# FFN up projection: weights as the loaded operand, tokens as the streamed one

## The reference, cut to what matters

```
D_FF, FFN_CONV = 5632, 3
hn = rmsnorm(h, norm_ffn_w)                       # 256 x 2048
up = causal_dwconv(hn @ w_up, conv_w, conv_b)     # w_up: 2048 x 11264, 3 taps along the tokens
gate, val = jnp.split(up, 2, axis=-1)
h = h + (jax.nn.silu(gate) * val) @ w_down        # w_down: 5632 x 2048
return rmsnorm(h, final_norm_w)
```

## Time and profile before

| | |
|---|---|
| median of 3 runs | 3444.38 us |
| the profiled execution | 3444.65 us |
| its span in the trace | 3442.9 us |
| TensorE matmul busy | 3421.1 us, 99% |
| VectorE busy | 2153.8 us, 63% |
| ScalarE busy | 1647.0 us, 48% |
| first up matmul to first down matmul | 2696.33 to 3194.21 us |

### The profile page before, as it was taken

How to read it: one execution, slowest core, us unless ns; L and a number is a source line. 1 busy time by engine, 2 the same in 40 slices (tenths; PEclk the granted TensorE clock), 3 DMA queues, 4 the chain that set the end, 5 groups by cost and what they waited for, 6 DMA issues and landing times.

```text
span 3442.9 us, 44116 instructions
## 1 busy us (share of the span) xinstructions
PE 3421.1 (99%) x16186; PEld 2791.2 (81%) x16186; DVE 2153.8 (63%) x2573; ACT 1647.0 (48%) x2159; POOL 218.6 (6%) x407
## 2 busy tenths in 40 slices
PE   8999999999999999999999999999999999999999
PEld 6777877778888877888888888888888888888887
DVE  5657577768687657565467774656545566666544
ACT  6442244543354245545555554444444566566433
POOL 1010100101100100100011000000000000000000
PEclk9999999999999999999999999999999999999999
DMA  9987635556867735657777676765655666666665
GB/s 377 398 288 270 223 123 187 176 186 234 271 201 247 272 114 183 235 189 213 216 235 235 211 237 206 250 215 188 206 168 158 186 185 185 186 185 183 202 195 166
DMA packets 331822, 738.85 MB, mean 215 GB/s; under 512 B 26423, under 2 KB 27025, under 8 KB 328448
## 3 DMA queue, kind: packets, MB, share of 16 engines
q1 hardware_dynamic: 298496, 620.83, 56.7%
q0 software_dynamic: 30640, 106.22, 8.7%
q10 hardware_dynamic: 2512, 9.45, 0.8%
HBM read 691.19 MB, written 45.21 MB: 214 GB/s over the span
## 4 chain that ended last, share of the span: by engine, by line
PE 98%; DVE 1%; ACT 1%; DMA 0%; issue 0%; POOL 0%; ACTq 0%; DVEq 0%; POOLq 0%
PE psum L734 30%; PE psum L736 29%; PE psum L735 29%; PE psum L1262 1%; PE psum L1281 1%; PE psum L560 1%; PE psum L1270 1%; PE psum L1325 1%; PE psum L2467 1%; PE psum L1310 0%; PE psum L806 0%; PE psum L2109 0%; PE psum L2277 0%; PE psum L2264 0%; PE psum L1966 0%; PE psum L1247 0%
## 5 line engine op out<-in xcount | busy, mean ns | idle before, releaser
L631 DVE TENSOR_TENSOR w_lo<-w_raw,w_hi 128x1024 fp32r<-128x1024 f32 x997 | 1217.5, 1224 | 1101.8 <-ACT w_hi L623 1099.1
L623 ACT ACTIVATE w_hi<-w_raw 128x1024 fp32r<-128x1024 f32 x997 | 1052.3, 1059 | 1283.2 <-PE psum L736 1169.7
L734 PE MATMUL psum<-w_hi,a_hi 128*128 128x512 f32 x3072 | 1216.0, 396 | 0.8 <-DVE w_lo L631 0.8
L736 PE MATMUL psum<-w_hi,a_lo 128*128 128x512 f32 x3072 | 1198.1, 390 | 0.0
L735 PE MATMUL psum<-w_lo,a_hi 128*128 128x512 f32 x3072 | 1196.4, 389 | 0.0
L734 PEld LDWEIGHTS psum<-w_hi,a_hi 128*128 128x128 f32 x3072 | 577.5, 188 | 122.9 <-issue 7.0
L736 PEld LDWEIGHTS psum<-w_hi,a_lo 128*128 128x128 f32 x3072 | 577.0, 188 | 122.4
L735 PEld LDWEIGHTS psum<-w_lo,a_hi 128*128 128x128 f32 x3072 | 577.7, 188 | 115.8
L734 PE MATMUL psum<-w_hi,f_hi 128*128 128x512 f32 x704 | 276.0, 392 | 0.0
L736 PE MATMUL psum<-w_hi,f_lo 128*128 128x512 f32 x704 | 274.2, 390 | 0.0
L735 PE MATMUL psum<-w_lo,f_hi 128*128 128x512 f32 x704 | 273.9, 389 | 0.0
(11 more groups left out here) (388 smaller groups left out, 2800.7 us busy)
## 6 DMA issues: line engine op xcount, KB each, us to landing
w_raw<-w_in SPq DMA_DIRECT2D x416, 512.0 KB, 4.4
ada_raw<-w_ada SPq DMA_DIRECT2D x176, 512.0 KB, 6.2
w_raw<-ffn_w_up SPq DMA_DIRECT2D x176, 512.0 KB, 3.7
w_raw<-w_out SPq DMA_DIRECT2D x96, 512.0 KB, 4.5
w_raw<-ffn_w_down SPq DMA_DIRECT2D x88, 512.0 KB, 4.8
p<-stage POOLq DMA_DIRECT2D x152, 256.0 KB, 4.8
w_raw<-xa_w_k SPq DMA_DIRECT2D x32, 512.0 KB, 9.6
w_raw<-xa_w_v SPq DMA_DIRECT2D x32, 512.0 KB, 8.4
```

The source lines that it names most:

```text
L623: nc.scalar.activation(w_hi[:, slot], raw_of(k), ACT.Copy).then_inc(hi_ready, 1)
L631: nc.vector.tensor_tensor(w_lo[:, slot], raw_of(k), w_hi[:, slot].bitcast(F32), ALU.subtract).then_inc(lo_ready, 1)
L734: nc.tensor.matmul(acc, g.hi[:, tt, kt, :], w_hi[:, slot, kk, :], start=first, stop=False)
L736: mm = nc.tensor.matmul(acc, g.lo[:, tt, kt, :], w_hi[:, slot, kk, :], start=False, stop=last)
```

## The change

The up product gets a loop of its own in `up_pe`. For a piece it makes 24 matmuls: for each of four blocks of 128 output features and each of two row blocks, a 128x128 block of the weight piece (`w_hi` or `w_lo`) is loaded, and the 256 tokens of `f_hi` or `f_lo` are streamed, as two runs of 128. Two feature blocks share a bank, 256 columns each. The output has features on partitions. The transposes of `turn` are gone, as are its waits on ScalarE and on the convolution.

ScalarE's two copies per chunk are gone. At the end of a chunk VectorE multiplies each of the two banks (128x512) with `rs_row`, a row of the 256 token factors repeated on all partitions, into `stage`. The convolution reads `stage` instead of banks 4 to 7. `rs_row` is made once, in the first chunk: VectorE spreads each tile's factors over 128 columns, TensorE transposes the two squares into bank 4, VectorE copies the bank.

```diff
+        rs_row = at("rs_row", 206.25, [P, SEQ])
+        rs_spread = at("rs_spread", 202, [P, XT, P])
...
+        def up_half(c, f):
+            return stage[:, bank_of(UP, c, f // 2), 256 * (f % 2):256 * (f % 2) + 256]
...
 # ScalarE, conv and body
-                        act.wait_ge(ff_T, i * 4 + (2 * c + f // 2 + 1))
+                        act.wait_ge(acc_evac[bank_of(UP, c, f // 2)], evacs_of(UP, i, c, f // 2) + 1)
...
-                        nc.scalar.activation(y_ff[:, c, f, :], half(4 + 2 * c, f), ACT.Identity, bias=cw[:, c, 3, f:f + 1],
+                        nc.scalar.activation(y_ff[:, c, f, :], up_half(c, f), ACT.Identity, bias=cw[:, c, 3, f:f + 1],
...
-                    for tt in range(XT):
-                        bank = bank_of(UP, c, tt)
-                        wait_unit(act, UP, i, c, tt)
-                        if not first:
-                            act.wait_ge(ff_T, i * 4 - 4 + 2 * c + 2)
-                        nc.scalar.activation(stage[:, bank], psum[:, bank], ACT.Copy, scale=ffn_rs[:, 12 + tt:13 + tt]).then_inc(acc_evac[bank], 1)
 # VectorE, conv and body
-                            ins = nc.vector.scalar_tensor_tensor(y_ff[:, c, f, s:SEQ], half(4 + 2 * c, f)[:, 0:SEQ - s],
+                            ins = nc.vector.scalar_tensor_tensor(y_ff[:, c, f, s:SEQ], up_half(c, f)[:, 0:SEQ - s],
...
+                        if first and c == 0 and j == UP.per_chunk - 1:
+                            dve.wait_ge(late_done, 3)
+                            for tt in range(XT):
+                                ins = nc.vector.tensor_copy(rs_spread[:, tt], ffn_rs[:, 12 + tt:13 + tt].to_broadcast([P, P]))
+                            ins.then_inc(ff_row, 1)
                         split_lo(dve, UP, i, c * UP.per_chunk + j)
                         next(steps, None)
+                    if first and c == 0:
+                        dve.wait_ge(ff_row, 2)
+                        link(nc.vector.tensor_copy(rs_row[:], psum[:, 4, 0:SEQ]))
+                    for pair in range(2):
+                        bank = bank_of(UP, c, pair)
+                        wait_unit(dve, UP, i, c, pair)
+                        nc.vector.tensor_tensor(stage[:, bank].rearrange("p (f q) -> p f q", f=2), psum[:, bank].rearrange("p (f q) -> p f q", f=2),
+                                                rs_row[:].unsqueeze(1).to_broadcast([P, 2, SEQ]), ALU.mult).then_inc(acc_evac[bank], 1)
 # TensorE
-            def turn(i):
...
-                        for tt in range(XT):
-                            mm = nc.tensor.transpose(half(4 + 2 * c, f)[:, tt * P:(tt + 1) * P], stage[:, bank_of(UP, c, tt), f * P:(f + 1) * P], ident[:])
...
+            def piece(i, c, j):
+                k = c * UP.per_chunk + j
+                slot = UP.at(k) % RING
+                pe.wait_ge(lo_ready, i * UP.body_pieces + (UP.at(k) + 1 + RING))
+                for f in range(4):
+                    bank = bank_of(UP, c, f // 2)
+                    acc = psum[:, bank, 256 * (f % 2):256 * (f % 2) + 256].rearrange("p (t q) -> p t q", t=XT)
+                    if j == 0 and f % 2 == 0:
+                        pe.wait_ge(acc_evac[bank], evacs_of(UP, i, c, f // 2))
+                    for kk in range(2):
+                        kt = 2 * j + kk
+                        hi, lo = (w[:, slot, kk, f * P:(f + 1) * P] for w in (w_hi, w_lo))
+                        first, last = kt == 0 and f % 2 == 0, kt == UP.kt - 1
+                        nc.tensor.matmul(acc, hi, f_hi[:, :, kt, :], start=first, stop=False, skip_group_check=True)
+                        nc.tensor.matmul(acc, hi, f_lo[:, :, kt, :], start=False, stop=False, skip_group_check=True)
+                        mm = nc.tensor.matmul(acc, lo, f_hi[:, :, kt, :], start=False, stop=last, skip_group_check=True)
+                    if f == 3:
+                        mm.then_inc(ring_used, 1)
+                    elif f == 1 and j == UP.per_chunk - 1:
+                        mm.then_inc(acc_ready, 1)
...
+                    if first and c == 0:
+                        pe.wait_ge(ff_row, 1)
+                        for tt in range(XT):
+                            mm = nc.tensor.transpose(psum[:, 4, tt * P:(tt + 1) * P], rs_spread[:, tt], ident[:])
+                        mm.then_inc(ff_row, 1)
```

More of the change, by code:

```diff
@@ L273, in build_program @@
             sem(f"x_{n}") for n in ("sc", "bias", "exp", "p", "pT", "pcopied", "o", "hi", "lo"))
-        ff_T, ff_y, ff_conv, ff_silu, ff_g, ff_hi, ff_lo, ff_w = (sem(f"ff_{n}") for n in ("T", "y", "conv", "silu", "g", "hi", "lo", "w"))
+        ff_row, ff_y, ff_conv, ff_silu, ff_g, ff_hi, ff_lo, ff_w = (sem(f"ff_{n}") for n in ("row", "y", "conv", "silu", "g", "hi", "lo", "w"))
         late_sq, late_sum, late_rms, late_done = (sem(f"late_{n}") for n in ("sq", "sum", "rms", "done"))
@@ L2454, in up_pe @@
         def up_pe(pe, opening):
-            def turn(i):
[L2457 to L2460, removed]
-                            for tt in range(XT):
-                                pe.wait_ge(acc_evac[bank_of(UP, c, tt)], evacs_of(UP, i, c, tt) + 1)
-                            pe.wait_ge(ff_conv, i * 2 + (c + 1))
-                        for tt in range(XT):
-                            mm = nc.tensor.transpose(half(4 + 2 * c, f)[:, tt * P:(tt + 1) * P], stage[:, bank_of(UP, c, tt), f * P:(f + 1) * P], ident[:])
-                        if f % 2:
-                            mm.then_inc(ff_T, 1)
-                    yield
+            def piece(i, c, j):
[18 more added lines that the diff above has]
+                        mm.then_inc(acc_ready, 1)
@@ L2472, in body @@
             def body(i):
                 first = isinstance(i, int) and i == 0
-                steps = opening if first else turn(i - 1)
                 for c in range(2):
-                    chunk_pe(pe, UP, i, c, steps)
+                    for j in range(UP.per_chunk):
+                        piece(i, c, j)
+                        if first:
+                            next(opening, None)
+                    if first and c == 0:
[3 more added lines that the diff above has]
+                        mm.then_inc(ff_row, 1)
@@ L2477, in up_pe @@
             pairs(pe, body, UP.loops, 1)
             def last():
-                yield from turn(UP.loops - 1)
-                for _ in range(16):
+                for _ in range(19):
                     yield
```

## The result

The changed kernel takes 3452.89 us, the kernel before beside it on the same chip 3444.92 us, 13 runs each: ratio 1.0024, 95% interval [1.0016, 1.0032]. It is slower by 8.0 us; the forecast was 3453.4 us.

A forecast was written before the change was run, and what follows sets the result against it. TensorE, busy 99% of the span, was taken to bound the kernel through its instructions' number and spacing. -19.4 + 28.2 + 0.2 = +9.0 us on the profiled execution gave a forecast of 3453.4 us, range 3427 to 3468 us.

The forecast's parts named there:

- What bounds the kernel: Whole kernel: TensorE busy 99% of the span at 2.4 GHz throughout, so only its instructions' number and spacing count.
- Transposes, -19.4 us: Up product: removing 22 blocks of eight transposes, 0.88 us each, saves 19.4 us.
- Matmuls, 120.0 ns and +28.2 us: Up product: 4224 matmuls of 256 columns at 120.0 ns replace 2112 of 512 columns, 478.7 us becoming 506.9.
- one matmul of 0.39 us: The L736 at 483.93 us, without a load beneath, lasts as long; so the load beneath doesn't make the fp32r excess.
- fixed 13.3 ns: Up product: each matmul costs its streaming plus 13.3 ns whatever its length, giving 120.0 ns; chance 0.50.
- comparison of L806 with L1325: Plain fp32 matmuls of 128 and 256 columns: excess 2.7 and 2.4 ns, so it goes with the instruction, not the columns.
- rs_row, +0.2 us: First chunk of the up product: two added transposes on TensorE at 0.11 us each, their source ready; +0.2 us.
- VectorE and ScalarE, 0: Up loop: VectorE's four added multiplications, 2.7 us per turn, stay behind TensorE's lead and ScalarE loses four; 0 us.
- delays at piece edges: Up product: small TensorE delays between pieces, 0.06 us of a turn, left unchanged in the forecast.
- Proportional excess: Up product, rival: excess goes with streamed columns, 113.3 ns a matmul, 3425.2 us; chance 0.27, whole or in part.
- Load and excess added, 122.3 ns: Up product, rival: the load sets the pace with the fp32r excess on top, +37.9 us, 3463.1 us; chance 0.16.
- Another wait: Up loop, rival: VectorE's new place or instruction fetch makes TensorE wait, one us per turn, 3464 us; chance 0.07.

The follow-up runs named there:

- 384-column run: Kernel before with 384 of the 512 columns streamed in each up-product matmul, a quarter of the output columns left out; 3332.77 us in one run.
- first alternating form: Changed kernel with `w_hi` streaming `f_hi` and `f_lo` as 512 columns, `w_lo` streaming `f_hi` as 256, in turn; median 3448.67 us, ratio 1.0004.
- form with one run of 512: The first alternating form with the 512 streamed columns laid out as one contiguous run and a shorter wait for `rs_row`; 3445.61 us, ratio 1.0003.
- wide form: Changed kernel with `f_hi` and `f_lo` side by side, streamed by `w_hi` in one 512-column matmul; here the first alternating form, 3448.67 us.

## Why the prediction was right, step by step

**What bounds the kernel.** Held. TensorE's starts follow each other without a gap in both kernels, and every run that kept its count and spacing kept the time, the doubled multiplications on VectorE included. One reading was too wide: the clock was not at 2.4 GHz throughout. The page shows the clock as one digit for each of 40 slices of some 86 us, which hides the stretch at 1.2 GHz from 1324.5 to 1327.9 us. It lies outside the up product and changes no term.

**Transposes, -19.4 us.** Measured alone, -19.6. Two of the 22 blocks stand behind the up stage, in the down product, so the stage itself, from the first up matmul to the first down matmul, grew by 10.1 us (497.9 to 507.9, in the changed kernel from 2695.85 to 3203.79 us) and 1.8 us came off after it. The other 0.5 us between the two spans lie ahead of the stage, where nothing was changed; there the trace before has its stretch at 1.2 GHz, and the trace after has none.

**Matmuls, 120.0 ns and +28.2 us.** The spacing is 120.0 ns, and the length alone costs +27.3 us. The number was right and one reason for it was wrong. I argued from one matmul of 0.39 us with nothing beneath it that the excess isn't made by the load and "belongs to the matmul". That row excluded too little: the matmul still had a full load of its own ahead, as every fp32r matmul in the trace had. With 64 columns loaded the excess is 6.7 ns. A fixed 13.3 ns held because the change kept 128 columns loaded for each matmul, at full clock; as far as the forecast leant on that row, it was luck. What carried it was the comparison of L806 with L1325: the streamed columns halve, the full load stays, the excess stays. That is the case of this change, and the 384-column run confirms it.

**rs_row, +0.2 us.** From the last matmul before the two transposes at 2719.62 to the second after at 2720.08 us are 0.46 us, of which two matmuls are 0.24: +0.2. TensorE didn't wait for their source.

**VectorE and ScalarE, 0.** Held: 684 ns a multiplication against 680 to 683 forecast, no turn with a gap.

**The sum.** +9.0 forecast, +8.0 measured; 0.7 us of the difference are the delays at piece edges, which the dense new order no longer has (46.08 us a turn is 384 x 120.0 ns exactly). The remaining 0.3 us are within what sets of runs of the kernel before differ by (medians of 3444.38 to 3444.95).

**The rivals.** Proportional excess: refuted by 173.3 and 120.0 ns. Load and excess added, 122.3 ns: refuted by 120.0; the floor of a load and the stream with its excess don't add, the longer counts. Another wait: none in either turn shown, with all 384 spacings filling the 46.08 us.

## What to carry to other kernels

When operand roles are swapped, count the matmuls with their loads, not only the streamed columns: in fp32r at 2.4 GHz each matmul with a full load cost 13.3 ns above its stream, and with 192 columns the spacing was 111.7 ns, not 93.3. A stream of 256 columns pays 12.5% where one of 512 pays 6%. Taking out transposes that TensorE makes is worth their time only if the new form keeps the streamed length; putting two streamed operands that share a loaded one side by side is a way to keep it. Group equal lengths. Before calling a cost fixed per instruction, ask what all the instructions at hand have in common; here it was the full load.

## What the runs showed of the hardware that I had not expected

- The excess of an fp32r matmul over its streaming was 13.3 ns with 128 columns loaded and 6.7 ns with 64, at 256 streamed columns (the output narrowed with the load). At the 1.2 GHz level there was none: 512 columns, 426.7 ns.
- Alternating 512 and 256 columns cost 6.7 ns a pair (353.3 against 346.7), grouping by two 1.7 (348.3). Why is not shown. The 11 runs of the first alternating form reach from 3439.91 to 3450.89 us, where the kernel before beside it had 3444.25 to 3445.98; 9.3 us is what 6.7 ns a pair makes, so some executions may run without it. The 11 of the form with one run of 512 reach only from 3444.84 to 3446.53. There is no trace of a short execution, and this stays open.
- With streams of 128 columns the granted clock moved between its two levels, with a mean of 0.64 and 0.69 in the two windows above, and at the 1.2 GHz level the spacing, which I read as paced by the load, was 213 ns. In the first turn of the wide form it fell to 1.2 GHz after a wait of 2.78 us.
